# Grouped attention's first weights, tables and norm vector loaded during the last expert before it, and its output weights in sixteen pieces

## The reference, cut to what matters

```python
def _gqa_axial(h, w_qkv, g_qn, g_kn, w_o, row, col):
    proj = h @ w_qkv                                   # 1024 -> 16 q, 8 k and 8 v heads of 128
    q = _axial_rope(_rms(q, g_qn), row, col)
    k = _axial_rope(_rms(k, g_kn), row, col)
    o = _block_attention(q, k, v, HD ** -0.5)          # softmax(q k^T) v, two q heads to a k head
    return o.reshape(b, s, HB * HD) @ w_o

x = x + _gqa_axial(_rms(x, g_attn_b[j]), ...)
x = x + _ec_moe(_rms(x, g_ffn[i]), ...)                # gate, up and down matrices of 16 experts
```

## Time and profile before

| what | before |
|---|---|
| median of 3 runs | 2383.52 us (2380.80 to 2385.99) |
| the profiled execution's own time | 2383.84 us |
| its span, first to last instruction | 2382.1 us |
| mean granted TensorE clock, as a share of full speed | 0.955 |
| matmuls, busy | 2147.7 us, 90% of the span |
| DVE / ACT / POOL busy | 1666.1 / 1337.5 / 719.6 us |
| DMA, mean over the span | 218 GB/s |

### The profile page before, as it was taken

One profiled execution on the slowest core, in us unless ns is written; L12 is line 12 of the kernel. 1 busy time (PEld: TensorE's weight loads), 2 busy tenths in 40 slices (PEclk: granted clock), 3 DMA queues, 4 the chain that ended last, 5 costly groups with the idle time before them and its releaser, 6 DMA issues. The chain is left out here.

```text
span 2382.1 us, 31773 instructions
## 1 busy us (share of the span) xinstructions
PE 2147.7 (90%) x10404; PEld 1611.0 (68%) x10404; DVE 1666.1 (70%) x1944; ACT 1337.5 (56%) x1678; POOL 719.6 (30%) x622
## 2 busy tenths in 40 slices
PE   8898887969999999985899999959959999999993
PEld 5566665747777777764688888848847777777772
DVE  3577774578888888864566666543268888888883
ACT  3366653147777777753444445442117777777772
POOL 1243331012332333215445444420001333234222
PEclk9899998979999999997999999979979999999997
DMA  7000004859999999935111111053279999999973
GB/s 267 2 13 12 12 13 137 294 207 385 377 383 391 387 377 387 393 97 155 43 49 52 50 49 51 14 218 108 71 271 356 391 376 386 395 379 381 388 293 128
DMA packets 183868, 520.39 MB, mean 218 GB/s; under 512 B 13088, under 2 KB 66080, under 8 KB 183520
## 3 DMA queue, kind: packets, MB, share of 16 engines
q1 hardware_dynamic: 176608, 494.05, 55.3%
q0 software_dynamic: 7168, 25.17, 4.5%
HBM read 481.43 MB, written 37.75 MB: 218 GB/s over the span
## 5 line engine op out<-in xcount | busy, mean ns | idle before, releaser
L1887 DVE TENSOR_TENSOR m_w_lo<-s_raw,m_w_hi 128x2048 fp32r<-128x2048 f32 x384 | 865.8, 2288 | 144.8 <-ACT m_w_hi L1836 143.3
L1836 ACT ACTIVATE m_w_hi<-s_raw 128x2048 fp32r<-128x2048 f32 x384 | 731.4, 1917 | 175.6 <-PE m_ps_down L1932 77.1
L1807 POOL DMA_INDIRECT acc<-m_ye,m_row_scatter x32 | 47.0, 1470 | 688.3 <-ACT m_ye L1853 688.3
L1930 PE MATMUL m_ps_gate<-m_w_hi,m_xeT_hi 128*96 128x512 f32 x512 | 205.8, 402 | 3.8 <-DVE m_xeT_lo L1893 3.8
L1930 PE MATMUL m_ps_down<-m_w_hi,m_hidT_hi 128*96 128x512 f32 x512 | 203.7, 398 | 3.8 <-DVE m_hidT_lo L1893 3.8
L1932 PE MATMUL m_ps_gate<-m_w_hi,m_xeT_lo 128*96 128x512 f32 x512 | 204.0, 399 | 0.0
L1932 PE MATMUL m_ps_down<-m_w_hi,m_hidT_lo 128*96 128x512 f32 x512 | 204.0, 398 | 0.0
L1930 PE MATMUL m_ps_up<-m_w_hi,m_xeT_hi 128*96 128x512 f32 x512 | 203.8, 398 | 0.0
L1932 PE MATMUL m_ps_up<-m_w_hi,m_xeT_lo 128*96 128x512 f32 x512 | 202.5, 396 | 0.0
L1931 PE MATMUL m_ps_gate<-m_w_lo,m_xeT_hi 128*96 128x512 f32 x512 | 202.4, 395 | 0.0
L1931 PE MATMUL m_ps_down<-m_w_lo,m_hidT_hi 128*96 128x512 f32 x512 | 202.3, 395 | 0.0
(11 more groups left out here) (239 smaller groups left out, 4490.3 us busy)
## 6 DMA issues: line engine op xcount, KB each, us to landing
s_raw<-in_w_gate SPq DMA_DIRECT2D x128, 1024.0 KB, 7.8
s_raw<-in_w_up SPq DMA_DIRECT2D x128, 1024.0 KB, 7.5
s_raw<-in_w_down SPq DMA_DIRECT2D x128, 1024.0 KB, 8.1
s_raw<-in_w_qkv_b SPq DMA_DIRECT2D x16, 512.0 KB, 5.1
s_raw<-in_w_qkv_b SPq DMA_DIRECT2D x32, 256.0 KB, 5.8
s_raw<-in_w_o_b SPq DMA_DIRECT2D x1, 8192.0 KB, 23.0
acc<-o_x SPq DMA_DIRECT2D x12, 512.0 KB, 2.9
xn<-o_xn SPq DMA_DIRECT2D x12, 512.0 KB, 3.0
```

The lines of the kernel that those rows point to most:

```text
L1807: pool.indirect_dma_start(out=io.acc, out_offset=bass.IndirectOffsetOnAxis(ap=row_scatter[:, :], axis=0), in_=ye[:, :], in_offset=None, co ...
L1836: act.activation(hi[:, split, :, :].rearrange("p k n -> p (k n)"), raw[:, slot, :], ACT.Copy).then_inc(hi_ready, 1)
L1887: dve.tensor_tensor(lo[:, split, :, :].rearrange("p k n -> p (k n)"), raw[:, slot, :], hi[:, split, :, :].rearrange("p k n -> p (k n)"), A ...
L1930: pe.matmul(out[:, cols], left_hi[:, k, :], hi[:, split, kk, cols], start=(k == 0), stop=False)
```

## The change

Two edits, both in SP's stream and in the waits that go with it.

First, the norm vector, the first group's weights, the rotation tables and the two gains of the grouped attention are loaded at the end of SP's stream in `moe_block` of layer 0, behind the last expert's down matrix, into slots 4 to 7 (ten transfers, which wait for the splits of the gate matrix that lay there). They signal semaphores that outlive the block. In `gqa_block` SP then issues only the x tiles, and the second group's weights wait for the norm of all six tiles too (`xn_ready`, 6), since the norm vector now lies where they go. It lay in slot 11 before.

Second, the one transfer of `w_o_b` becomes sixteen of 128 x 1024 numbers (512 KB): three before each of the first five stores of the last group, and one before the sixth. `output_block` waits for all of them.

```diff
@@ gqa_block, SP
             for t in range(2):
                 sp.dma_start(norm.x[:, t % 2, :], norm.x_tile_of(t)).then_inc(norm.x_landed[t], 16)
-            sp.dma_start(norm.gain, norm.gain_row).then_inc(norm.gain_landed, 16)
-            weights(0, 0, 0)
-            weights(0, 0, 1)
-            sp.dma_start(rope, io.rope_b).then_inc(tables_landed, 16)
-            sp.dma_start(gains[:, 0, :], row_broadcast(io.g_qn_b[0])).then_inc(tables_landed, 16)
-            sp.dma_start(gains[:, 1, :], row_broadcast(io.g_kn_b[0])).then_inc(tables_landed, 16)
             for t in range(2, TILES):
                 sp.wait_ge(norm.xn_ready, t - 1)
                 sp.dma_start(norm.x[:, t % 2, :], norm.x_tile_of(t)).then_inc(norm.x_landed[t % 2], 16)
             sp.wait_ge(tables_ready, 15)
+            sp.wait_ge(norm.xn_ready, TILES)
             weights(1, 1, 0)
             weights(1, 1, 1)
...
-            def stores(g):
+            def stores(g, between=None):
                 for unit in range(NU):
+                    if between:
+                        between(unit)
                     core.store(sp, g, unit, rows_of)
+
+            def load_w_o(unit):
+                for k in range(3 * unit, min(3 * unit + 3, HEADS)):
+                    sp.dma_start(shared.w_o_b[:, k, :], io.w_o_b[0, k * P:(k + 1) * P, :]).then_inc(shared.w_o_landed, 16)
...
             sp.wait_ge(proj_done, NU * GROUPS)
-            sp.dma_start(shared.w_o_b, io.w_o_b[0].rearrange("(k p) n -> p k n", p=P)).then_inc(shared.w_o_landed, 16)
-            stores(GROUPS - 1)
+            stores(GROUPS - 1, load_w_o)
@@ moe_block, SP
             step(LAST)
+            if layer == 0:
+                for j in range(4):
+                    wait_low(sp, LAST - 1, 4 + j)
+                sp.dma_start(shared.norm_gain, row_broadcast(io.g_attn_b[0])).then_inc(shared.gain_landed, 16)
+                for h in range(2):
+                    shared.load_qkv(sp, 0, 0, h, shared.qkv_landed[h])
+                sp.dma_start(shared.rope, io.rope_b).then_inc(shared.tables_landed, 16)
+                sp.dma_start(shared.gains[:, 0, :], row_broadcast(io.g_qn_b[0])).then_inc(shared.tables_landed, 16)
+                sp.dma_start(shared.gains[:, 1, :], row_broadcast(io.g_kn_b[0])).then_inc(shared.tables_landed, 16)
```

More of the change, by code:

```diff
@@ L106, with __init__ @@
 class InputNorm:
-    def __init__(self, s, x_tile_of, gain_row, xnT, psum, x, xn, junk, gain, xnT_lo=None):
+    def __init__(self, s, x_tile_of, gain_row, xnT, psum, x, xn, junk, gain, xnT_lo=None, gain_landed=None):
         self.x_tile_of, self.gain_row, self.xnT, self.ps = x_tile_of, gain_row, xnT, psum
@@ L901, in gqa_block @@
         HALF_K = KD // 2
-        w_raw = arena[:, 4 * SLOT:8 * SLOT].rearrange("p (b k n) -> p b k n", b=2, k=KD)
+        w_raw = shared.w_qkv
         w_lo = shared.over_raw(nc, "b_w_lo", [P, 2, KD, W], 4)
         w_hi = shared.over_raw(nc, "b_w_hi", [P, 2, KD, W], 8)
-        rope = arena[:, 6 * SLOT:6 * SLOT + TILES * 2 * HD].rearrange("p (t a n) -> p t a n", a=2, n=HD)
-        gains = arena[:, 7 * SLOT:7 * SLOT + 2 * HD].rearrange("p (g n) -> p g n", g=2)
+        rope, gains = shared.rope, shared.gains
         squares = arena[:, 0:3 * HD].rearrange("p (h n) -> p h n", h=3)
@@ L942, in gqa_block @@
                          junk=junk,
-                         gain=arena[:, at_x + 2 * D:at_x + 3 * D], xnT_lo=xnT_lo)
+                         gain=shared.norm_gain, xnT_lo=xnT_lo, gain_landed=shared.gain_landed)
         first_turns = core.T[:, :, :, :].rearrange("p b k n -> p b (k n)")
         w_landed = [s.sem("w_landed0"), s.sem("w_landed1")]
-        tables_landed, tables_ready = s.sem("tables_landed"), s.sem("tables_ready")
+        tables_landed, tables_ready = shared.tables_landed, s.sem("tables_ready")
         half_ready, w_high, w_split = s.sem("half_ready"), s.sem("w_high"), s.sem("w_split")
@@ L962, in weights @@
                     sp.wait_ge(proj_done, g * NU - NU)
[L963 to L971, removed]
+                sp.wait_ge(w_split, g * 2 - 1 + h)
+                shared.load_qkv(sp, g, slot, h, w_landed[h])
             for t in range(2):
                 sp.dma_start(norm.x[:, t % 2, :], norm.x_tile_of(t)).then_inc(norm.x_landed[t], 16)
-            sp.dma_start(norm.gain, norm.gain_row).then_inc(norm.gain_landed, 16)
-            weights(0, 0, 0)
-            weights(0, 0, 1)
-            sp.dma_start(rope, io.rope_b).then_inc(tables_landed, 16)
-            sp.dma_start(gains[:, 0, :], row_broadcast(io.g_qn_b[0])).then_inc(tables_landed, 16)
-            sp.dma_start(gains[:, 1, :], row_broadcast(io.g_kn_b[0])).then_inc(tables_landed, 16)
             for t in range(2, TILES):
@@ L1068, in split_high @@
             def split_high(g, slot, h):
-                act.wait_ge(w_landed[h], g * 48 + 48)
+                if isinstance(g, int) and g == 0:
+                    act.wait_ge(shared.qkv_landed[h], 48)
+                else:
+                    act.wait_ge(w_landed[h], g * 48)
                 if not (isinstance(g, int) and g < 2):
@@ L1470, in exp @@
                                ACT.Exp).then_inc(exp_ready, 1)
-            act.wait_ge(shared.w_o_landed, 16 * (layer + 1))
+            act.wait_ge(shared.w_o_landed, 16 if layer == 0 else 16 + 16 * KO)
             for k in range(4):
@@ L2061, in __init__, with load_qkv @@
         self.w_o_b = arena[:, (SLOTS - 8) * SLOT:].rearrange("p (k n) -> p k n", n=D)
+        self.w_qkv = arena[:, 4 * SLOT:8 * SLOT].rearrange("p (b k n) -> p b k n", b=2, k=KD)
+        self.rope = arena[:, 6 * SLOT:6 * SLOT + TILES * 2 * HD].rearrange("p (t a n) -> p t a n", a=2, n=HD)
+        self.gains = arena[:, 7 * SLOT:7 * SLOT + 2 * HD].rearrange("p (g n) -> p g n", g=2)
+        self.norm_gain = arena[:, 7 * SLOT + 2 * HD:7 * SLOT + 2 * HD + D]
     def over_raw(self, nc, name, shape, first_slot):
         return nc.alloc_sbuf_tensor_at(name, shape, F32R, offset=self.raw_at + first_slot * SLOT * 4)
+    def load_qkv(self, sp, g, slot, h, landed):
+        half_k = KD // 2
+        src = self.io.w_qkv_b[0].rearrange("(h k p) n -> h p k n", h=2, p=P)[h]
+        dst = self.w_qkv[:, slot, h * half_k:(h + 1) * half_k, :]
+        sp.dma_start(dst[:, :, 0:2 * HD], src[:, :, bass.ds(g * 2 * HD, 2 * HD)]).then_inc(landed, 16)
+        sp.dma_start(dst[:, :, 2 * HD:3 * HD], src[:, :, bass.ds(g * HD + HEADS * HD, HD)]).then_inc(landed, 16)
+        sp.dma_start(dst[:, :, 3 * HD:],
+                     src[:, :, bass.ds(g * HD + (HEADS + KV_HEADS) * HD, HD)]).then_inc(landed, 16)
     def load_first(self, sp, matrix, layer, first_slot, j):
```

4 lines of the change are left out of this document (3 added, 1 removed).

## The result

| | before | after |
|---|---|---|
| median, runs side by side | 2384.76 us (2380.80 to 2386.00, 4 runs) | 2369.35 us (2368.52 to 2370.08, 4 runs) |
| ratio, 95% interval | | 0.9938 [0.9924, 0.9952] |
| profiled execution's own time | 2383.84 us | 2368.52 us |
| its span | 2382.1 us | 2366.7 us |
| mean granted TensorE clock | 0.955 | 0.959 |

A forecast was written before the change was run, and what follows sets the result against it. TensorE, 90% busy, was taken to bound the kernel, with gains only where it stands still. 6.0 us at the start and 8.1 at the end, 14.1 off 2383.84, gave 2369.7 us, range 2363 to 2377.

The forecast's parts named there:

- The wait at the start: Start of grouped attention: TensorE no longer waits for x tile 2 and goes on at 1101.5 instead of 1106.11, 4.6 us.
- The clock behind that wait: Start of grouped attention: without the wait, turn and projection take 6.61 us instead of 8.04, 1.4 us.
- What is late next: Start of grouped attention: the rotation of tile 0 is late next, moves along with TensorE, and is given no gain.
- The ports: Rival, start: GpSimd's tables meet the weight splits, VectorE pays 1.83 us, low clock stays; 2.8 us, so 2372.9; chance 0.10.
- What was costed at nothing: Ten early transfers in the last expert and the second group's later weights: no cost.
- The wait at the end: Last group: ScalarE copies unit 2 out at 1566.67 instead of 1573.63, no longer waiting for the store, 7.0 us.
- The rest of the end: Last group: three units take 17.4 us instead of 18.45, without the wait that let the clock fall, 1.1 us.
- The slow pieces: Rival, end: pieces go one at a time at 3.2 us each, end loses 17.1 us, so 2394.9; chance 0.04.
- The sum: Whole change: 6.0 us at the start and 8.1 us at the end, 14.1 us together.

The follow-up runs named there:

- the end alone: Changed kernel with the ten early transfers put back in the grouped attention behind x tiles 0 and 1, the sixteen pieces kept: 2377.51 us.
- the two experiments on pieces: Changed kernel with all sixteen pieces issued ahead of the last group's six stores: 2376.99 us; changed kernel with thirty-two pieces of 256 KB between the stores: 2370.34 us.
- the start alone: Changed kernel with the output weights as one transfer again, the early first loads kept: 2377.38 us.
- the heads later: Changed kernel with the rotation of tile 0's heads behind tile 4's multiplication and tile 3's low copy, their turn behind x tile 4's: 2365.79 us.

## Why the prediction was right, step by step

**The wait at the start** (4.6 us forecast) gave 5.73 to the third turn. Its parts: the projection began 1.57 us earlier (1.7 forecast), the 2.92 us of waiting went whole, and 1.24 us came that the sum did not have. The step that failed is "TensorE's first projection took 8.54 us", carried over unchanged: it took 7.30. The granted clock rises inside it, and in the changed kernel it does so sooner. The windows of the projection before (us, busy by engine, PEclk, DMA share, GB/s):

```profile
1094.65:1100.35 5.70, 5.70 (x14) 4.44 (x15) 2.29 (x1) 3.28 (x6) 5.03 (x4) 0.50 0.35 137
1100.35:1103.20 2.85, 2.83 (x12) 2.00 (x10) 1.16 (x1) 0.00 (x0) 2.68 (x5) 0.96 0.00 0
```

and after:

```profile
1092.10:1095.50 3.40, 3.40 (x8) 2.73 (x9) 2.63 (x2) 2.28 (x5) 3.20 (x4) 0.50 0.02 5
1095.50:1099.40 3.90, 3.90 (x17) 2.91 (x17) 3.75 (x2) 0.00 (x0) 3.90 (x4) 0.99 0.12 17
```

The lower level holds for 5.70 us of it before and 3.40 after; each stretch times its clock, the two projections are the same work (5.6 us at full clock), so the clock accounts for the whole difference. Ahead of it TensorE did the same two turns with waits in both. With the start undone (the end alone) the projection takes 1106.09 - 2.71 - 1094.95 = 8.43 us; in all runs with an edit at the start it takes 7.3 to 7.6. So it belongs to the first edit; what makes the clock rise sooner no run here singles out.

**The clock behind that wait** (1.4 us forecast): turn and projection took 6.51 us instead of 8.04, 1.53 us. With no wait before them the granted clock was 1.00 over these 6.51 us; over the 8.04 it was 0.79.

**What is late next.** The forecast had VectorE done with tile 2 at 1099.3 and TensorE at 1101.5. VectorE was done at 1098.04 + 1.21 = 1099.25, and TensorE at 1099.40. Measured from the block's start VectorE was 1 us later than forecast, mostly because 1/rms of tile 2 came 1.7 us late. Tile 2's square was done on time (14.55 us into the block, 14.74 forecast). The tables were done some 2 us later than forecast (14.52 into the block), but still no later than the square. What the sum did not have is the first step of the norm behind them: on 128 numbers it took 2.08 us instead of 0.19, beside VectorE's second split, and it ended at 1094.60 with that split (1094.55). The forecast had 2.2 us to spare at this place. The lateness and the shorter projection used up all but 0.15 us of them, so that TensorE did not wait was partly luck, and a still faster projection would wait again.

**The ports** (0.10) were felt, but not where that rival had them. VectorE's two splits took 4.92 us where the kernel with the end alone, whose tables come later, has 4.59; that is 0.3 us, not an instruction of 1.83 us. GpSimd paid. The tables began 4.3 us before the splits, not early enough to be done ahead of them: the four instructions of 128x192 took 5.28 us, and in the end-alone kernel, behind the splits, 2.25, as the two timelines (VectorE, GpSimd) of that one show:

```profile
1092.52 4.59 DVE L1143 TENSOR_TENSOR b_w_lo<-s_raw,b_w_hi 128x2048 fp32r<-128x2048 f32 x2 [0.57 <-ACT b_w_hi L1074]
```

```profile
1098.76 2.25 POOL L1024 TENSOR_TENSOR b_tables<-s_raw 128x192 f32<-128x192 f32 x4
```

In the changed kernel two of the four took about 0.58 us each. The first met the multiplication of tile 1 and took 1.57, and the last began 0.13 us behind the first split and ended 0.45 behind it:

```profile
1089.76 2.64 POOL L1018 TENSOR_TENSOR b_tables<-s_raw 128x192 f32<-128x192 f32 x1
```

The rule of the Trainium skill that the prediction named ("SBUF — State Buffer", section "SBUF: two separate sides") says that one instruction blocks the other for its whole length. The traces agree for the pair at tile 1 (2.75 and 1.81 us against 1.28 and 2.79) and for GpSimd's two steps that end with VectorE's splits (2.64 and 2.08 us); that the shared ports are the cause was not tested by itself.

**What was costed at nothing** cost nothing that shows. The early transfers are issued from 1033.48 on, in the last expert, 44 us ahead of the block, and TensorE works through that stretch without a gap:

```profile
1033.48:1043.99 10.51, 10.51 (x47) 7.29 (x46) 8.81 (x5) 8.46 (x5) 1.32 (x1) 1.00 1.03 331
```

The second group's weights are issued at 1119.98 instead of 1112.85, by the new wait, and ScalarE splits them at 1138.45 without waiting (1146.75 before).

**The wait at the end** (7.0 us forecast) gave 6.98: unit 2 follows unit 1 after 5.77 us instead of 12.75. **The rest of the end** (1.1 us) did not come. The three units from there took 18.71 us, 18.45 before, against 17.4 forecast. The failed step is "a unit takes 5.79 us, three 17.4", put down to the low clock that the store's wait had caused. The windows of these units after, whole and at their slowest:

```profile
1558.36:1577.07 18.71, 13.54 (x72) 11.67 (x70) 6.92 (x14) 7.14 (x18) 4.49 (x5) 0.82 0.67 235
1563.40:1572.40 9.00, 7.17 (x33) 6.35 (x33) 2.81 (x6) 2.80 (x7) 3.17 (x4) 0.69 0.72 264
```

The clock did come back in part, 0.82 against 0.69, and the time did not. One reason is in the counts of matmuls, 72 after and 62 in the window of before. While ScalarE waited for the store, TensorE went on with the next unit's scores and half of a turn, as the window of that wait before shows:

```profile
1566.61:1573.63 7.02, 1.81 (x11) 1.27 (x9) 1.39 (x2) 0.00 (x0) 0.45 (x1) 0.86 0.90 355
```

So the three units before had a head start of 1.81 us of TensorE's work and 1.39 of VectorE's, which goes when the wait goes; the forecast set 17.4 us against their 18.45 without it. The other reason is that each unit waits for more than the clock. TensorE waits once in each unit for the low part of the probabilities. TensorE's waits from 1558.36 to 1577.07 after (us in total, times, longest):

```profile
PE b_ps_probsT L259 <- DVE b_probsT_lo L345: 5.1, 3, 1.8
```

and from 1573.63 to 1592.08 before:

```profile
PE b_ps_probsT L259 <- DVE b_probsT_lo L345: 4.7, 3, 1.8
```

These waits are no shorter with the higher clock, and behind the first of them the clock falls without a store's help: 0.69 from 1563.40 on. The units also differ in length by themselves: after unit 2 they take 6.35, 7.73 and 4.63 us, and 6.00, 7.75 and 4.70 before, so that the 5.77 us from unit 1 to unit 2 were no measure for the others. How much of the 1.1 us each of these takes isn't separated. The rows of the two units before that the earlier trace rows leaves out:

```profile
1579.63 0.39 ACT L305 ACTIVATE s_raw<-b_ps_probsT 128x256 f32<-128x256 f32 x1 [2.40 <-PE b_ps_probsT L261]
1587.38 0.39 ACT L305 ACTIVATE s_raw<-b_ps_probsT 128x256 f32<-128x256 f32 x1 [2.33 <-PE b_ps_probsT L261]
```

**The slow pieces** (0.04) fall with the two experiments on pieces: sixteen in a row would have held the first store back for 16 x 3.2 = 51 us, and it came after 24. The 3.2 us that one transfer takes alone are shared when several are in flight. The Trainium skill's advice of at least 1 MiB for a transfer ("DMA: Bandwidth & Descriptors", section "Rules for kernel authors") would have spoken against the edit; here smaller ones cost nothing that shows, 24.48 us for four units with 512 KB and 24.44 with 256 KB.

**The sum** was 14.1, and the two places gave 7.26 + 6.72 = 13.98. That it fits so well is luck: the start gave 1.3 us more than forecast and the end 1.4 less, and the two errors cancelled. The last 1.4 us of the spans' difference are the block's earlier start (0.98) and what lies behind. The block began at 1077.88 in the changed kernel, and between 1078.33 and 1080.51 in the four others that have exactly the same work ahead of it (the start alone, the two experiments on pieces, the heads later). So the 0.98 lies within the scatter between executions.

## What to carry to other kernels

A small store that an engine waits for should have no more bytes ahead of it on its queue than land while the engine works; when a large load must share that queue, cut it and put the pieces between the stores; here thirty-two pieces were as quick as sixteen. Loads that the first instructions of a block need can go into the block before, where there is room for them and time on the queue; here the large ones were what mattered, and with them gone the small ones could stay. A gain carried over from one unit of a loop to the next needs the loop's own waits looked up first, and what the other engines get done during the wait that is to go.

## What was not expected of the hardware

- Two engines that start a two-input instruction within 0.2 us of each other: the first keeps its time (1.81 us on GpSimd, 1.28 on VectorE), the second takes 2.75 (VectorE) or 2.79 (GpSimd).
- GpSimd's single norm step on 128 numbers took 2.08 us beside VectorE's split and ended 0.05 us behind it; at the later tiles it took 0.19.
- The granted clock rose 3.40 us into the first projection instead of 5.70, and the projection was 1.24 us shorter.
- Thirty-two transfers of 256 KB between the stores left the units where sixteen of 512 KB had them, 24.44 and 24.48 us from unit 1 to unit 5.
